# One 512-column matmul for the two that share a tile's high weights

## The chip, the core and the metric

The kernel runs on one core of a Trainium2 chip. The metric is device time in microseconds (us) of one execution. PE is TensorE, DVE is VectorE, ACT is ScalarE, POOL is GpSimd and SP is the engine that issues the loads. The core has an SBUF for tiles and a PSUM of banks of 512 fp32 columns, into which TensorE writes its products.

## The reference

Two blocks of a language model over 256 tokens of width 2048. The first holds a pooling layer and a sparse-attention layer, the second one attention layer of three kinds of heads and a gated feed-forward layer of width 5632. All inputs and outputs are fp32. Most of the arithmetic is in projections of this kind:

```python
h = rmsnorm(x, norm_g)
proj = h @ w_in                                   # 2048 x 4096 and more
return x + jnp.concatenate([y_pool, y_mem], -1) @ w_out
...
hid = silu(dwconv(h @ w_gate)) * (h @ w_up)       # 2048 x 5632 each
x = x + hid @ w_down
```

## The kernel before

Activations stand transposed: 16 blocks of 128 features by T = 256 tokens. A weight comes as 699 units of up to 128x1024 fp32 (8 blocks of 128x128). Each unit passes a stage: SP loads it into one of four slots (`s_stage`), ACT rounds it to fp32r (`s_wh`, line 1059), and DVE subtracts to get the low part (`s_wl`, line 1574). There are three slots for each of the two parts, so ACT waits until TensorE is done with the unit three before. Every activation block has a high and a low part too, `R[:, 0, k, :]` and `R[:, 1, k, :]` (`s_rh`, `s_ry`, `s_hid`). A product is then the sum of three matmuls of 256 columns per block (lines 490 to 492): high weights with high activations, high weights with low ones, low weights with high ones. I call the three matmuls of one 128x128 weight block a k-tile.

Most output tiles have two units, so 16 k-tiles, and lie in one of two PSUM banks (`psg`) in turn; groups of four tiles use two banks more (`pst`). In the residual stages (`wo0`, `wo1`, `wo2`, `wd`) some first tiles (4, 8, 12 and 2 of 16) go in passes: one pass takes one unit of each of these tiles, the next pass the other. `pair` computes values with 512 moving columns (lines 549 to 551) and isn't touched by the change except that it waits for both banks.

DVE takes every tile out of its bank: `scaled` (lines 1620 and 1622) multiplies it with the row norm, `add` (line 1793) adds it to the residual `X`. The order on each engine is written out by hand: `nxt()` runs one step of the side jobs and then one split of a unit. In the last pass of a residual stage DVE's order for each tile is add, low part of the new activation (line 1592), split of a unit; ACT's is high part (line 1071), rounding of a unit. `held` and `vacant` make TensorE wait for the bank until the tile that lay in it has been taken out (semaphore `out`). POOL sums squares of X for the norms (lines 2263 to 2270; for `wo1` also 2512 to 2519) and builds the windows of the compressed keys (line 2343).

Of the kernel before, what the change touches and what calls it, by code (L numbers as in the profile page):

```python
# [466 lines left out]


def both(R):
    return lambda k: (R[:, 0, k, :], R[:, 1, k, :])  # L470


def tensor_program(e, S, P, M):
# [4 lines left out]
    def vacant(*banks):  # L478

        for b in banks:  # L480
            if b in held:
                w.wait_ge(*held[b])

    def unit():
        done[0] += 1
        side.tick()

    def three(o, wh, wl, x, first, last):
        xh, xl = x
        e.matmul(o, wh, xh, start=first, stop=False)  # L490
        e.matmul(o, wh, xl, start=False, stop=False)  # L491
        return e.matmul(o, wl, xh, start=False, stop=last)  # L492

    def ready(name, base=0):
        return lambda k: w.wait_ge(name + "l", base + k + 1)

    def b_unit(o, nk, k0, first, last, x, ready, mw=128):
        c = done[0]
        r = c % NR
        w.wait_ge("wl", c + 1)  # L500
        for kk in range(nk):
            ws = slice(kk * mw, kk * mw + mw)
            ready(k0 + kk)
            m = three(o, M.WH[:, r, ws], M.WL[:, r, ws], x(k0 + kk), first and kk == 0, last and kk == nk - 1)
        m.then_inc(S["units"], 1)

    def tile(t, x, ready, sizes=(8, 8), k0=0, mw=128):

        bank = P.bank[t]
        vacant(bank)  # L510
        held[bank] = P.out[t]
        k = k0
        for n, nk in enumerate(sizes):
            b_unit(M.product(bank)[0:mw, 0:T], nk, k, n == 0, n == len(sizes) - 1, x, ready, mw)
            k += nk
            if n == len(sizes) - 1:
                assert done[0] + 1 == P.end[t], t
            unit()

    def group(tiles, x, ready, hook=None):  # L520

        for n in range(2):
            for p, t in enumerate(tiles):
                if n == 0:
                    vacant(P.bank[t])
                    held[P.bank[t]] = P.out[t]
                b_unit(M.product(P.bank[t])[:, 0:T], 8, 8 * n, n == 0, n == 1, x, ready)
                if hook is not None and n == 0 and p == 3:
                    hook()
                unit()  # L530

    def pair(t, x, ready):

        banks = [P.bank[t, i] for i in range(2)]
        vacant(*banks)
        for i in range(2):
            held[banks[i]] = P.out[t, i]
        for u in range(8):
            c = done[0]
            r = c % NR  # L540
            w.wait_ge("wl", c + 1)
            steps = [(kk, i) for i in range(2) for kk in range(2)] if u == 7 else [(kk, i) for kk in range(2) for i in range(2)]
            for n, (kk, i) in enumerate(steps):
                k = 2 * u + kk
                ready(k)
                xh, xl = x(k)
                ts, ws = slice(128 * i, 128 * i + 128), slice(512 * kk, 512 * kk + 512)
                o = M.product(banks[i])
                e.matmul(o[:, :], xh[:, ts], M.WH[:, r, ws], start=(k == 0), stop=False)  # L549
                e.matmul(o[:, :], xh[:, ts], M.WL[:, r, ws], start=False, stop=False)  # L550
                m = e.matmul(o[:, :], xl[:, ts], M.WH[:, r, ws], start=False, stop=(k == 15))  # L551
                if u == 7 and n == 1:
                    m.then_inc(S["half"], 1)
            m.then_inc(S["units"], 1)
            unit()

    def residual(name, x, ready, order=(0, 1), early=4, sizes=(8, 8)):
        at = [sum(sizes[:m]) for m in range(len(sizes))]
        for n, m in enumerate(order):
            for j in range(early):  # L560
                tile((name, j) if n == len(order) - 1 else (name, "part", m, j), x, ready, (sizes[m],), at[m])
        for j in range(early, KT):
            tile((name, j), x, ready, sizes)
# [69 lines left out]
    def pool_group(g):  # L633
        for i in range(3):
            tile(("z", 3 * g + i), H0, ready("h0"))
        for a, nt in ((0, 2), (2, 1)):
            c = done[0]
            r = c % NR
            w.wait_ge("wl", c + 1)
            w.wait_ge("rpl", g + 1)  # L640
            for i in range(a, a + nt):
                bank = ("t", 0) if i == 2 else ("o", i)
                o = M.PST[:, 0, 0:T] if i == 2 else M.PSO[i][:, 0:T]
                vacant(bank)
                for k in range(3):
                    ws = slice(((i - a) * 3 + k) * 128, ((i - a) * 3 + k + 1) * 128)
                    m = three(o, M.WH[:, r, ws], M.WL[:, r, ws], (M.RP[g % 2][:, 0, k, :], M.RP[g % 2][:, 1, k, :]), k == 0, k == 2)
                if i == 0:
                    m.then_inc(S["wp0"], 1)
                held[bank] = ("y_w", YAT["pool"] + 3 * g + i + 1)  # L650
            m.then_inc(S["units"], 1)
            if a == 2:
                side.tick()
            unit()
# [226 lines left out]
    def diff_head(h):  # L881
# [149 lines left out]
    for hv in range(2):  # L1031
        first = 22 * hv
        if hv == 0:
            group([(n, j) for j in range(2) for n in ("wg", "wu")], Y, ready("hf"), ffn_hook)
            first = 2
        for j in range(first, 22 * hv + 22):
            tile(("wg", j), Y, ready("hf"))
            tile(("wu", j), Y, ready("hf"))
        residual(("wd", hv), both(M.HID), ready("hid", 22 * hv), (0, 1, 2), 2, (8, 7, 7))
# [523 lines left out]
def vector_program(e, S, P, M):  # L1563
# [12 lines left out]
    def nxt(n=1):  # L1576
        for _ in range(n):
            side.tick()
            split()

    def chain(ins):

        ins.then_inc(S["dve"], 1)
        chained[0] += 1

    def link():
        w.wait_ge("dve", chained[0])
# [25 lines left out]
    def whole(t):  # L1613
        w.wait_ge("units", P.end[t])
        return M.product(P.bank[t])

    def scaled(t, dst, scale, rb):

        if scale is None:
            e.tensor_tensor(dst, whole(t)[:, 0:T], M.RB[rb][:, :], ALU.mult).then_inc(S["out"], 1)  # L1620
        else:
            e.scalar_tensor_tensor(dst, whole(t)[:, 0:T], scale, M.RB[rb][:, :], ALU.mult, ALU.mult).then_inc(S["out"], 1)

    def tiles(name, n, dst, scale, rb):
        for j in range(n):
# [18 lines left out]
    def silu(*t):  # L1644
        i = ZAT[t]
        yield
        yield
        w.wait_ge("z_t", i + 1)
        if t[0] == "zm":
            dst = (M.ZS0, M.ZS1)[t[1]][t[2] % 4]  # L1650
        else:
            dst = M.ZS0[t[1] % 4] if t[0] == "z" else M.ZS1[t[1] % 4]
        e.scalar_tensor_tensor(dst[:, :], M.ET[i % 2][:, :], 1.0, M.ZT[i % 2][:, :], ALU.add, ALU.mult).then_inc(S["z_d"], 1)

    def gate(rb, *t):

        nxt()
        i = ZAT[t]
        if i >= 2:
            w.wait_ge("z_d", i - 1)  # L1660
        e.scalar_tensor_tensor(M.ZT[i % 2][:, :], whole(t)[:, 0:T], 0.5, M.RB[rb][:, :], ALU.mult, ALU.mult).then_inc(S["out"], 1)
        side.start(silu(*t))
        nxt()

# [125 lines left out]

    def add(t, j):

        e.tensor_tensor(M.X[:, j, :], whole(t)[:, 0:T], M.X[:, j, :], ALU.add).then_inc(S["out"], 1)  # L1793

    def residual(name, post, order=(0, 1), early=4, units=2, begin=None):
        for n, m in enumerate(order):
# [85 lines left out]
    def gates():  # L1882
        yield
        yield
        w.wait_ge("gt_act", 1)
        gf = M.GT[:, :, :].rearrange("p t c -> p (t c)")
        chain(e.tensor_scalar(gf, gf, 1.0, None, ALU.add))
        link()
        e.reciprocal(gf, gf).then_inc(S["gts"], 1)
# [166 lines left out]
    side.start(mem_norm())  # L2056
    nxt(4)
    for j in range(4):
        e.tensor_copy(M.MK0[:, j, :], whole(("mk", 0, j))[:, 0:T]).then_inc(S["out"], 1)
        nxt()  # L2060
    v_pair(("mv", 0), M.MV0[:, 0, :], 0, "mem_c")
    side.start(x_low())
# [59 lines left out]
        if j % 2:  # L2122
            side.start(rope_pair(5 + j // 2, M.QN, j))
    w.wait_ge("hct", 2)
    e.tensor_tensor(M.ZT[0][0:36, :], whole("gate")[0:36, 0:T], M.RB[0][0:36, :], ALU.mult).then_inc(S["out"], 1)
    side.start(gates())
    nxt()
    for j in range(4):
# [71 lines left out]
    for hv in range(2):  # L2200
        first = 22 * hv
        if hv == 0:
# [9 lines left out]
            first = 2  # L2212
# [22 lines left out]
    for n, (a, b) in enumerate(((0, 1), (1, 3), (3, 6), (6, 9), (9, 11))):  # L2235
        w.wait_ge("xg", b)
        for j in range(a, b):
            x = e.tensor_tensor(M.X[:, j, :], M.X[:, j, :], M.RB[1][:, :], ALU.mult)
# [490 lines left out]
```

## Time and profile before

| | us |
|---|---|
| three runs, median (lowest to highest) | 2176.29 (2176.24 to 2177.77) |
| the profiled execution, its own time | 2176.39 |
| its span in the profile | 2174.6 |
| PE busy | 2123.9 |
| DVE busy | 1272.6 |
| ACT busy | 990.4 |
| POOL busy | 575.1 |

A matmul's record of some 284 ns overlaps the next ones, so the busy time of PE says only that it had work; the pace is read from the starts of two matmuls. Times of rows are from the span's start.

### The profile page before, as it was taken

To read this page: it belongs to the slowest core of one execution; us is meant where nothing else is said; L and a number is where in the kernel's file an instruction comes from. 1 tells how busy PE (TensorE), PEld (TensorE's weight loads), DVE (VectorE), ACT (ScalarE), POOL (GpSimd) and SP (SyncE) were. 2 spreads that over 40 slices of the span, in tenths; PEclk is the share of its full clock that TensorE was granted. 3 is DMA by queue.
4 is the path that set the end of the run, shared out by engine and by line. 5 is a ranking of instruction groups with operands and counts; after the bars stand their busy time and mean duration, and the time that the engine had idled before them with its cause. 6 is when DMAs were issued, how large, how long until landed. Compare 5 with 4: busy or idle time off the path is not lost.

```text
span 2174.6 us, 38858 instructions
## 1 busy us (share of the span) xinstructions
PE 2123.9 (98%) x16462; PEld 2040.3 (94%) x16462; DVE 1272.6 (59%) x1667; ACT 990.4 (46%) x1428; POOL 575.1 (26%) x551
## 2 busy tenths in 40 slices
PE   7999999999899999989999999999999999999997
PEld 7899999998799999989978899999999999999997
DVE  8855665566655545656545556666555455655544
ACT  5544444444532545433455454454444334444443
POOL 8214442233400244691121122311110001111122
PEclk9999999999999999999999999999999999999998
DMA  7554555556654433565554445656656665655664
GB/s 251 174 184 146 188 181 191 176 178 190 192 180 125 134 107 109 167 197 171 157 162 140 127 135 160 191 180 181 184 184 180 180 192 182 181 183 183 180 181 133
DMA packets 104126, 370.61 MB, mean 170 GB/s; under 512 B 11633, under 2 KB 12945, under 8 KB 103825
## 3 DMA queue, kind: packets, MB, share of 16 engines
q1 hardware_dynamic: 103952, 368.13, 54.5%
q8 instruction: 130, 2.13, 0.4%
q14 instruction: 44, 0.35, 0.0%
HBM read 365.98 MB, written 2.10 MB: 169 GB/s over the span
## 4 chain that ended last, share of the span: by engine, by line
PE 88%; POOL 6%; DVE 3%; ACT 1%; issue 1%; DMA 0%; SPq 0%; DVEq 0%; POOLq 0%; ACTq 0%
PE psg L490 24%; PE psg L491 24%; PE psg L492 24%; POOL s_zf L2343 2%; PE psg L549 2%; PE psg L550 2%; PE psg L551 2%; DVE s_wl L1574 1%; POOL s_psq L2267 1%; POOL s_psq L2512 1%; PE pst L492 1%; PE pst L491 1%; PE pst L490 1%; POOL s_psq L2517 1%; PE pst L586 1%
## 5 line engine op out<-in xcount | busy, mean ns | idle before, releaser
L1574 DVE TENSOR_TENSOR s_wl<-s_stage,s_wh 128x1024 fp32r<-128x1024 f32 (+3 forms) x699 | 864.9, 1239 | 553.9 <-ACT s_wh L1059 551.8
L1059 ACT ACTIVATE s_wh<-s_stage 128x1024 fp32r<-128x1024 f32 (+3 forms) x699 | 726.3, 1041 | 774.9 <-PE psg L492 686.7
L490 PE MATMUL psg<-s_ry,s_wh 128*128 128x256 f32 x2672 | 765.0, 286 | 2.9 <-DVE s_mv L1635 2.5
L491 PE MATMUL psg<-s_ry,s_wh 128*128 128x256 f32 x2672 | 757.9, 284 | 0.0
L492 PE MATMUL psg<-s_ry,s_wl 128*128 128x256 f32 x2672 | 757.7, 284 | 0.0
L490 PEld LDWEIGHTS psg<-s_ry,s_wh 128*128 128x128 f32 x2672 | 513.5, 192 | 11.7 <-issue 5.5
L491 PEld LDWEIGHTS psg<-s_ry,s_wh 128*128 128x128 f32 x2672 | 513.4, 192 | 0.5
L492 PEld LDWEIGHTS psg<-s_ry,s_wl 128*128 128x128 f32 x2672 | 513.3, 192 | 0.1
L490 PE MATMUL psg<-s_rh,s_wh 128*128 128x256 f32 x1280 | 369.8, 289 | 12.4 <-DVE s_rh L1592 10.2
L492 PE MATMUL psg<-s_rh,s_wl 128*128 128x256 f32 x1280 | 363.8, 284 | 0.0
L491 PE MATMUL psg<-s_rh,s_wh 128*128 128x256 f32 x1280 | 363.8, 284 | 0.0
L490 PEld LDWEIGHTS psg<-s_rh,s_wh 128*128 128x128 f32 x1280 | 247.0, 193 | 17.1 <-issue 11.3
L491 PEld LDWEIGHTS psg<-s_rh,s_wh 128*128 128x128 f32 x1280 | 247.2, 193 | 0.4
L492 PEld LDWEIGHTS psg<-s_rh,s_wl 128*128 128x128 f32 x1280 | 247.1, 193 | 0.0
L2426 POOL TENSOR_TENSOR s_hid<-s_hh,s_hid 128x256 fp32r<-128x256 f32 x44 | 64.5, 1465 | 575.9 <-ACT s_hid L1397 575.9
L490 PE MATMUL psg<-s_hid,s_wh 128*128 128x256 f32 x704 | 199.2, 283 | 0.0
L491 PE MATMUL psg<-s_hid,s_wh 128*128 128x256 f32 x704 | 199.2, 283 | 0.0
L492 PE MATMUL psg<-s_hid,s_wl 128*128 128x256 f32 x704 | 199.2, 283 | 0.0
L490 PEld LDWEIGHTS psg<-s_hid,s_wh 128*128 128x128 f32 x704 | 135.2, 192 | 0.0
L491 PEld LDWEIGHTS psg<-s_hid,s_wh 128*128 128x128 f32 x704 | 135.2, 192 | 0.0
L492 PEld LDWEIGHTS psg<-s_hid,s_wl 128*128 128x128 f32 x704 | 135.2, 192 | 0.0
L2267 POOL TENSOR_TENSOR s_psq<-s_x 128x256 f32<-128x256 f32 x74 | 58.4, 789 | 165.0 <-DVE s_x L1793 162.8
(378 smaller groups left out, 2388.5 us busy)
## 6 DMA issues: line engine op xcount, KB each, us to landing
s_stage<-in_wo SPq DMA_DIRECT2D x96, 512.0 KB, 3.4
s_stage<-in_wg SPq DMA_DIRECT2D x88, 512.0 KB, 3.5
s_stage<-in_wu SPq DMA_DIRECT2D x88, 512.0 KB, 3.5
s_stage<-in_ain SPq DMA_DIRECT2D x64, 512.0 KB, 3.3
s_stage<-in_wd SPq DMA_DIRECT2D x64, 448.0 KB, 3.4
s_stage<-in_wkv SPq DMA_DIRECT2D x32, 512.0 KB, 3.7
s_stage<-in_wd SPq DMA_DIRECT2D x32, 512.0 KB, 3.6
s_stage<-in_bq SPq DMA_DIRECT2D x24, 512.0 KB, 3.5
```

What stands on the lines that cost most here:

```text
L490: e.matmul(o, wh, xh, start=first, stop=False)
L491: e.matmul(o, wh, xl, start=False, stop=False)
L492: return e.matmul(o, wl, xh, start=False, stop=last)
L549: e.matmul(o[:, :], xh[:, ts], M.WH[:, r, ws], start=(k == 0), stop=False)
L550: e.matmul(o[:, :], xh[:, ts], M.WL[:, r, ws], start=False, stop=False)
L551: m = e.matmul(o[:, :], xl[:, ts], M.WH[:, r, ws], start=False, stop=(k == 15))
L586: m = e.transpose(M.PST[:, h, b:b + 128], src[:, a:a + 128], ident)
L1059: e.activation(M.WH[:, c % NR, 0:n], M.ST[:, c % NS, 0:n], ACT.Copy).then_inc(S["wh"], 1)
L1574: e.tensor_tensor(M.WL[:, c % NR, 0:n], M.ST[:, c % NS, 0:n], M.WH[:, c % NR, 0:n], ALU.subtract).then_inc(S["wl"], 1)
L2267: chain(e.tensor_tensor(b, src, src, ALU.mult))
L2343: x = e.tensor_scalar(dst, Z[:, :, l:l + 16 * 14 + 1:16], M.vec("pe", 32 * v + l), None, ALU.add)
L2426: e.tensor_tensor(M.HID[:, 1, i, :], M.HH[j % 2][:, :], M.HID[:, 0, i, :].bitcast(F32), ALU.subtract).then_inc(S["hidl"], 1)
```

## The change

The high and low parts of an activation block are taken as one moving operand of two runs of 256 columns, so that the high weights are used in one matmul of 512 columns. It fills both halves of a bank: columns 0 to 255 get high by high, 256 to 511 high by low. The low weights' matmul of 256 columns adds to the second half. In the last k-tile of a tile it comes first, so that the wide one ends the tile. DVE adds the halves: `scaled` by a reduction over pairs of columns that lie 256 apart, then the multiplication as a second instruction that waits for the first; `add` by two additions in a row.

```diff
 def both(R):
-    return lambda k: (R[:, 0, k, :], R[:, 1, k, :])
+    return lambda k: (R[:, 0, k, :], R[:, :, k, :], R[:, 1, k, :])
...
-            m = three(o, M.WH[:, r, ws], M.WL[:, r, ws], x(k0 + kk), first and kk == 0, last and kk == nk - 1)
+            xh, xx, _ = x(k0 + kk)
+            begin, end = first and kk == 0, last and kk == nk - 1
+            if end:
+                e.matmul(o[:, T:2 * T], M.WL[:, r, ws], xh, start=False, stop=False)
+            m = e.matmul(o, M.WH[:, r, ws], xx, start=begin, stop=end)
+            if not end:
+                m = e.matmul(o[:, T:2 * T], M.WL[:, r, ws], xh, start=False, stop=False)
         m.then_inc(S["units"], 1)
...
+    def summed(t, dst, rows=128):
+        return e.tensor_reduce(dst, whole(t)[0:rows, :].rearrange("p (s t) -> p t s", s=2), AX.X, ALU.add)
+
-    def scaled(t, dst, scale, rb):
+    def scaled(t, dst, scale, rb, rows=128):
+        chain(summed(t, dst, rows))
+        link()
         if scale is None:
-            e.tensor_tensor(dst, whole(t)[:, 0:T], M.RB[rb][:, :], ALU.mult).then_inc(S["out"], 1)
+            e.tensor_tensor(dst, dst, M.RB[rb][0:rows, :], ALU.mult).then_inc(S["out"], 1)
...
     def add(t, j):
-        e.tensor_tensor(M.X[:, j, :], whole(t)[:, 0:T], M.X[:, j, :], ALU.add).then_inc(S["out"], 1)
+        b = whole(t)
+        chain(e.tensor_tensor(M.X[:, j, :], b[:, T:2 * T], M.X[:, j, :], ALU.add))
+        link()
+        e.tensor_tensor(M.X[:, j, :], b[:, 0:T], M.X[:, j, :], ALU.add).then_inc(S["out"], 1)
...
-        e.tensor_copy(M.MK0[:, j, :], whole(("mk", 0, j))[:, 0:T]).then_inc(S["out"], 1)
+        summed(("mk", 0, j), M.MK0[:, j, :]).then_inc(S["out"], 1)
```

On PE, near the end of a tile of the first group (memory keys, stationary blocks of `s_wh` and `s_wl`, bank `pst`), the order before is:

```order
L490 MATMUL pst<-s_rh,s_wh 128x256
L491 MATMUL pst<-s_rh,s_wh 128x256
L492 MATMUL pst<-s_rh,s_wl 128x256
L490 MATMUL pst<-s_rh,s_wh 128x256
L491 MATMUL pst<-s_rh,s_wh 128x256
L492 MATMUL pst<-s_rh,s_wl 128x256
```

and now:

```order
L508 MATMUL pst<-s_rh,s_wh 128x512
L510 MATMUL pst<-s_rh,s_wl 128x256
L508 MATMUL pst<-s_rh,s_wh 128x512
L510 MATMUL pst<-s_rh,s_wl 128x256
L507 MATMUL pst<-s_rh,s_wl 128x256
L508 MATMUL pst<-s_rh,s_wh 128x512 x2
```

A k-tile has two matmuls instead of three; at the tile's end two narrow ones stand in a row, then the wide one of this tile and the wide one of the next.

On DVE, in the last pass of the stage `wo2` (one unit per tile), the order before is:

```order
L1793 TENSOR_TENSOR s_x<-psg,s_x 128x256
L1592 SCALAR_TENSOR_TENSOR s_ry<-s_x,s_vec,s_ry 128x256
L1574 TENSOR_TENSOR s_wl<-s_stage,s_wh 128x1024
L1793 TENSOR_TENSOR s_x<-psg,s_x 128x256
L1592 SCALAR_TENSOR_TENSOR s_ry<-s_x,s_vec,s_ry 128x256
```

and now:

```order
L1806 TENSOR_TENSOR s_x<-psg,s_x 128x256
L1808 TENSOR_TENSOR s_x<-psg,s_x 128x256
L1598 SCALAR_TENSOR_TENSOR s_ry<-s_x,s_vec,s_ry 128x256
L1580 TENSOR_TENSOR s_wl<-s_stage,s_wh 128x1024
L1806 TENSOR_TENSOR s_x<-psg,s_x 128x256
L1808 TENSOR_TENSOR s_x<-psg,s_x 128x256
```

Each tile has one addition more ahead of the low part and the split.

## Rows read from the trace of the kernel before

**Rows 1.** The page: the span and busy times.

```profile
span 2174.6 us, 38858 instructions
PE 2123.9 (98%) x16462; PEld 2040.3 (94%) x16462; DVE 1272.6 (59%) x1667; ACT 990.4 (46%) x1428; POOL 575.1 (26%) x551
```

**Rows 2.** The page: shares of the chain that ended last, by engine.

```profile
PE 88%; POOL 6%; DVE 3%; ACT 1%; issue 1%; DMA 0%; SPq 0%; DVEq 0%; POOLq 0%; ACTq 0%
```

**Rows 3.** Groups by line, PE, line 490: name, shapes, count, busy us, mean ns, idle.

```profile
L490 PE MATMUL psg<-s_ry,s_wh 128*128 128x256 f32 x2672 | 765.0, 286 | 2.9 <-DVE s_mv L1635 2.5 <-DVE s_vcc L1635 0.4
L490 PE MATMUL psg<-s_rh,s_wh 128*128 128x256 f32 x1280 | 369.8, 289 | 12.4 <-DVE s_rh L1592 10.2 <-DVE s_wl L1574 2.0
L490 PE MATMUL psg<-s_hid,s_wh 128*128 128x256 f32 x704 | 199.2, 283 | 0.0
L490 PE MATMUL pst<-s_ry,s_wh 128*128 128x256 f32 x96 | 27.4, 285 | 0.0
L490 PE MATMUL pst<-s_rh,s_wh 128*128 128x256 f32 x64 | 18.1, 283 | 0.0
```

**Rows 4.** Instructions in time, PE, 256 columns: start us, length us, what.

```profile
999.77 0.28 PE L490 MATMUL psg<-s_ry,s_wh 128*128 128x256 f32 x1
...
1002.65 0.28 PE L490 MATMUL psg<-s_ry,s_wh 128*128 128x256 f32 x1
```

**Rows 5.** Instructions in time, PE, 512 columns.

```profile
92.90 0.39 PE L551 MATMUL psg<-s_wh,s_ry 128*128 128x512 f32 x1
...
94.94 0.39 PE L551 MATMUL psg<-s_wh,s_ry 128*128 128x512 f32 x1
```

**Rows 6.** Groups by line and shape, DVE.

```profile
L1620 DVE TENSOR_TENSOR s_uu<-psg,s_rb 128x256 f32<-128x256 f32 x43 | 18.2, 424 | 24.1 <-PE psg L492 24.1
L1744 DVE TENSOR_REDUCE s_stat<-pss 128x2 f32<-128x512 f32 x20 | 13.6, 680 | 0.0
L2046 DVE TENSOR_TENSOR s_hh<-s_uu,s_cv 128x256 f32<-128x256 f32 x44 | 18.3, 415 | 0.0
L1686 DVE TENSOR_TENSOR s_mk<-s_mk,s_rb 128x256 f32<-128x256 f32 x4 | 3.4, 894 | 0.0
```

**Rows 7.** Instructions in time, DVE, two that wait for one another.

```profile
977.91 0.42 DVE L1598 SCALAR_TENSOR_TENSOR s_nw<-pso,s_rb 128x256 f32<-128x256 f32 x1 [10.76 <-ACT s_rb L1078]
978.37 0.42 DVE L1600 SCALAR_TENSOR_TENSOR s_nw<-s_nw,s_rb 128x256 f32<-128x256 f32 x1
```

**Rows 8.** Stretches of time: busy us and count of each engine, clock, DMA.

```profile
20.00:30.00 10.00, 9.43 (x79) 9.23 (x77) 10.00 (x12) 6.33 (x11) 9.53 (x13) 1.00 0.58 207
1500.00:1550.00 50.00, 50.00 (x419) 50.00 (x418) 29.17 (x39) 23.14 (x30) 6.75 (x5) 1.00 0.60 183
```

**Rows 9.** Instructions in time, DVE, last pass of `wo2`.

```profile
1344.74 0.42 DVE L1793 TENSOR_TENSOR s_x<-psg,s_x 128x256 f32<-128x256 f32 x1 [0.57 <-PE psg L492]
...
1347.84 0.42 DVE L1793 TENSOR_TENSOR s_x<-psg,s_x 128x256 f32<-128x256 f32 x1
1348.83 0.48 DVE L1592 SCALAR_TENSOR_TENSOR s_ry<-s_x,s_vec,s_ry 128x256 fp32r<-128x256 f32 x1 [0.58 <-ACT s_ry L1071]
1349.78 1.23 DVE L1574 TENSOR_TENSOR s_wl<-s_stage,s_wh 128x1024 fp32r<-128x1024 f32 x1 [0.46 <-ACT s_wh L1059]
...
1378.69 0.41 DVE L1793 TENSOR_TENSOR s_x<-psg,s_x 128x256 f32<-128x256 f32 x1
```

**Rows 10.** Instructions in time, POOL: the first square of `wo1`.

```profile
889.81 0.61 POOL L2263 TENSOR_TENSOR s_acc<-s_x 128x256 f32<-128x256 f32 x1 [7.05 <-DVE s_x L1793]
```

**Rows 11.** Instructions in time, PE: the norm after `wo1`.

```profile
974.87 1.19 PE L569 MATMUL pso<-s_acc,s_one 128*128 128x256 f32 x2 [7.26 <-issue]
```

**Rows 12.** Chain that ended last, in order of time: the windows of the compressed keys.

```profile
480.37 3.77 POOL s_zf L2343 x4
484.16 0.64 ACT s_zb L1216
484.82 0.70 DVE s_zb L1846
485.61 4.36 POOL s_zf L2343 x4
```

**Rows 13.** Instructions in time, PE: a `pair` behind a tile.

```profile
1014.18 0.47 PE L549 MATMUL psg<-s_wh,s_ry 128*128 128x512 f32 x1 [0.56 <-DVE s_kcc L1620]
```

More of the change, by code:

```diff
@@ L513, in tile @@
         for n, nk in enumerate(sizes):
-            b_unit(M.product(bank)[0:mw, 0:T], nk, k, n == 0, n == len(sizes) - 1, x, ready, mw)
+            b_unit(M.product(bank)[0:mw, :], nk, k, n == 0, n == len(sizes) - 1, x, ready, mw)
             k += nk
@@ L526, in group @@
                     held[P.bank[t]] = P.out[t]
-                b_unit(M.product(P.bank[t])[:, 0:T], 8, 8 * n, n == 0, n == 1, x, ready)
+                b_unit(M.product(P.bank[t])[:, :], 8, 8 * n, n == 0, n == 1, x, ready)
                 if hook is not None and n == 0 and p == 3:
@@ L545, in pair @@
                 ready(k)
-                xh, xl = x(k)
+                xh, _, xl = x(k)
                 ts, ws = slice(128 * i, 128 * i + 128), slice(512 * kk, 512 * kk + 512)
@@ L1615, in whole @@
         return M.product(P.bank[t])
-    def scaled(t, dst, scale, rb):
+    def summed(t, dst, rows=128):
[3 more added lines that the diff above has]
+        link()
         if scale is None:
-            e.tensor_tensor(dst, whole(t)[:, 0:T], M.RB[rb][:, :], ALU.mult).then_inc(S["out"], 1)
+            e.tensor_tensor(dst, dst, M.RB[rb][0:rows, :], ALU.mult).then_inc(S["out"], 1)
         else:
-            e.scalar_tensor_tensor(dst, whole(t)[:, 0:T], scale, M.RB[rb][:, :], ALU.mult, ALU.mult).then_inc(S["out"], 1)
+            e.scalar_tensor_tensor(dst, dst, scale, M.RB[rb][0:rows, :], ALU.mult, ALU.mult).then_inc(S["out"], 1)
     def tiles(name, n, dst, scale, rb):
@@ L1660, in gate @@
             w.wait_ge("z_d", i - 1)
-        e.scalar_tensor_tensor(M.ZT[i % 2][:, :], whole(t)[:, 0:T], 0.5, M.RB[rb][:, :], ALU.mult, ALU.mult).then_inc(S["out"], 1)
+        scaled(t, M.ZT[i % 2][:, :], 0.5, rb)
         side.start(silu(*t))
@@ L2124, in vector_program @@
     w.wait_ge("hct", 2)
-    e.tensor_tensor(M.ZT[0][0:36, :], whole("gate")[0:36, 0:T], M.RB[0][0:36, :], ALU.mult).then_inc(S["out"], 1)
+    scaled("gate", M.ZT[0][0:36, :], None, 0, 36)
     side.start(gates())
```

## The prediction, made before the changed kernel ran

> **What bounds the kernel now.** I read the page's busy times first [rows 1]: PE has work in 98% of the span, DVE in 59%, ACT in 46%. Then the chain of waits [rows 2]: 88% of it is PE, 6% POOL, 3% DVE. So TensorE's pace is the bound, and the few places where the chain is on POOL or DVE are those where a faster TensorE gains nothing. Next I read that pace in the instructions in order of time. Eight k-tiles, 24 matmuls of 256 columns, take 1002.65 - 999.77 = 2.88 us [rows 4], 120.0 ns each. Nine matmuls of 512 columns take 94.94 - 92.90 = 2.04 us [rows 5], 226.7 ns each. 256 columns more cost 106.7 ns, so a matmul is 0.4167 ns per column and 13.3 ns besides. That the line through two points gives exactly a column per cycle of the 2.4 GHz level speaks for reading the 13.3 ns as a price per matmul, each with weights of its own.
>
> **The gain on TensorE.** The change touches 2672 + 1280 + 704 + 96 + 64 = 4816 k-tiles [rows 3]. Each was 3 x 120.0 = 360.0 ns and becomes 226.7 + 120.0 = 346.7 ns. The columns are the same 768; one matmul with its weight load goes. That is 13.3 ns per k-tile, 0.107 us per unit of eight, 64.2 us in all if TensorE never waits longer than before. The trace has no wide matmul whose moving operand lies in two runs far apart, and none between narrow ones. Its cost is bounded by what it replaces: at most two narrow ones (240.0 ns, gain nil); at the other end by the columns alone (213.3 ns, gain 26.7 ns per k-tile, 128 us). I take 226.7 ns, the row of the same width.
>
> Here a page speaks against the change. The Trainium skill, "TensorE: Matmul & The Clock Gate", section "Back-to-back issue gap", puts a warm matmul at N/2.4 + 2.5 ns; by that a k-tile would go from 327.5 to 325.0 ns, and the sum would be a gain of 12 us, an estimate. The rows differ from it at both widths, 120.0 and 226.7 ns, and I go by the rows.
>
> **The cost on DVE.** Of the 317 added DVE instructions 205 are in `scaled` and 112 in `add`. A `scaled` was one instruction of 0.42 us; now a reduction of 512 PSUM columns, nearest row 0.68 us, and a multiplication in SBUF of 0.42 us [rows 6]. Instructions that wait for one another start 0.46 us apart when 0.42 us long [rows 7], so a link adds 0.04 us: 1.14 us instead of 0.42. That is 0.72 us more for each, 148 us in all. An `add` gets 0.46 us more: 52 us. In the feed-forward stage DVE is busy 29.17 of 50 us [rows 8], 3.4 us per tile of 5.76 us; it becomes 4.1 of 5.55 us. The bank is freed some 0.7 us later with a whole tile's 5.55 us of room. So this is hidden behind TensorE in the long stages. The reduction's shape is unknown (256 sums of two, 256 columns apart): below it can't be under the 0.42 us of one reading of 256 columns, above I bound it at three times the row, 2.0 us; even that gives 5.5 us per tile and just fits.
>
> The multiplication now reads two SBUF tensors. Of that form one row has 415 ns and one, at the start where POOL is 9.5 us of 10 busy, 894 ns [rows 6, 8]. The Trainium skill, "SBUF — State Buffer", section "Who interferes with whom", says that a DVE instruction with two SBUF inputs contends with a POOL instruction that reads SBUF. By that rule, the trace agrees, and `add`, with one input in PSUM, is spared.
>
> **Where it isn't hidden.** (a) The last pass of `wo2`: 12 tiles of one unit. Adds are 3.085 us apart, (1378.69 - 1347.84)/10 [rows 9], more than a unit's 2.88: add, ACT's high part, ACT's rounding, DVE's split and the next add follow one another. The first add of the pass had waited for TensorE by 0.57 us, so the slack was being eaten but lasted. Now the period is 3.085 + 0.46 = 3.545 us, against a unit of 2.77. Behind the add stand the low part and the split, and TensorE waits for the bank: tile 12 of the stage can start when add 10 is done, 0.57 + 10 x 3.545 + 0.90 = 36.9 us after the end of tile 0, where TensorE alone would need 11 x 2.773 = 30.5. I charge 6.1 us, leaving 0.3 for what it lacked before. In `wo0` with four such tiles the same sum gives 0.3.
>
> (b) `wo1`: POOL squares from 889.81 to TensorE's norm at 974.87, before which TensorE idles 7.26 us [rows 10, 11]. POOL sets this stretch. The gain of its 27 units (7 of the last pass, 16 of the tiles behind, 4 of the group) is lost, 2.9 us, and its first square starts 0.46 us later. The same lag as in (a), for eight tiles, is inside that idle time.
>
> (c) The start: from 20 to 30 us DVE is busy 10.00 of 10 us [rows 8], and I take it for the bound of the whole first group. Its 64 k-tiles gain nothing, 0.85 us, and the four reductions in place of copies add 4 x 0.26 = 1.0.
>
> (d) The compressed keys: a loop of POOL, ACT, DVE of 485.61 - 480.37 = 5.24 us [rows 12] sets the pace. About seven units gain nothing, 0.75, and DVE's longer queue and POOL's sharing may add 1.0.
>
> (e) `pair` behind a tile waits for the bank, 0.56 us [rows 13]; two such places get 0.72 us more each: 1.5.
>
> (f) The last add, ahead of the final norm: 0.46.
>
> (g) Places with slack under a microsecond that I can't see before, most of all around the last heads where DVE and ACT wait for one another: 2, between 0 and 10.
>
> The sum: 0.3 + 6.1 + 2.9 + 0.46 + 0.85 + 1.0 + 0.75 + 1.0 + 1.5 + 0.46 + 2 = 17.3 us. 64.2 - 17.3 = 46.9 us. The profiled execution took 2176.39 us, the span 2174.6 and 1.8 around it, and the median of the runs is 2176.29: 2176.4 - 46.9 = 2129.5, so I forecast 2130 us.
>
> **The rivals.** *DVE hides less.* If the reduction is much over 0.68 us or the splits come late in the attention stages, another 8 to 30 us of waits appear. For it: DVE runs its list in order, and the splits stand behind the longer `scaled`. Against: in the feed-forward stage DVE keeps over a quarter of its time free. The time would be 2138 to 2160.
>
> *The price isn't per matmul.* If most of the 13.3 ns is a wait that the sequence of narrow and wide keeps, and a k-tile saves only a fifth of it, 2.7 ns, the gain is 13 us. The stalls, with a period of 3.545 against a unit of 2.86, are some 12: 2175. For it stands that both widths were measured only among their own kind. A gain of this size is what the page named above would give.
>
> *The wide matmul's weights come late (slower).* Its weights must be loaded under a narrow matmul, and its operand lies in two runs. If the pair of matmuls then takes 360 ns or more, nothing is gained, and what stays are the costs of DVE: (a) 36.9 against 11 x 2.88 = 31.7, so 4.9 more; 0.46, 1.0, 1.0, 1.5, 0.46 and 2: about 11 us slower, 2188. It decides from 357.7 ns per k-tile on (11 us / 4816 = 2.3 ns). Against: before, too, every load lies under a narrow matmul at 120 ns.
>
> *The reduction bounds (slower).* At 3 us it would make a feed-forward tile 6.5 us, (6.5 - 5.76) x 88 = 65 us over before for these alone, less about 20 us gained in the residual stages: 2220. It decides from about 2.6 us.
>
> **Chances.** Forecast 0.78 (its own range 2117 to 2138); DVE hides less 0.11; the price isn't per matmul 0.04, three quarters of it within 0.2% and one slower; late weights 0.04; reduction 0.03. A measurement of this kernel tells 0.2%, 4.4 us, from no change. Faster 0.78 + 0.11 = 0.89, same 0.03, slower 0.01 + 0.04 + 0.03 = 0.08. The range is 2117, with few of the waits of (a) to (g) and a little more gain, to 2144, which takes in the nearer part of the second case.
>
> **What would show it.** Starts of narrow and wide matmul 120 and 227 ns apart, a k-tile of 0.347 us; 9632 matmuls in `tile` and `group` instead of 14448. DVE busy about 1470 us, the reduction 0.68 us. Adds of the last pass of `wo2` 3.5 us apart with TensorE waiting for them; an idle time before the norm of `wo1` that is shorter by the lag of its last pass but ends as late after the first square, 85 us. A k-tile of 0.36 us, or a reduction of over 2 us, would make it wrong.

## The result, and the profile after

The changed kernel takes 2157.61 us (median of four runs, 2157.39 to 2158.88), the kernel before 2176.49 beside it: a ratio of 0.9913, interval 0.9896 to 0.993. It is 18.9 us faster, where 46.9 were forecast; 2157.6 lies outside the range of 2117 to 2144. The page of its profiled execution, span and busy times, against [rows 1], and the chain that ended last, against [rows 2]:

```profile
span 2155.6 us, 29543 instructions
PE 2092.7 (97%) x11646; PEld 1775.3 (82%) x11646; DVE 1456.3 (68%) x1984; ACT 996.9 (46%) x1428; POOL 570.1 (26%) x551
PE 84%; POOL 6%; DVE 5%; issue 2%; ACT 2%; DMA 0%; DVEq 0%; SPq 0%; POOLq 0%; ACTq 0%
```

4816 matmuls are gone (16462 to 11646) and DVE has 184 us more work, near the forecast's 200. The chain, third line, is still PE's with 84% in place of 88% [rows 2]. So TensorE's pace is what to read next: instructions in order of time on PE, start and length in us.

```profile
1502.19 0.40 PE L508 MATMUL psg<-s_ry,s_wh 128*128 128x512 f32 x1
1502.42 0.28 PE L510 MATMUL psg<-s_ry,s_wl 128*128 128x256 f32 x1
1502.54 0.40 PE L508 MATMUL psg<-s_ry,s_wh 128*128 128x512 f32 x1
...
1505.37 0.40 PE L508 MATMUL psg<-s_ry,s_wh 128*128 128x512 f32 x1
```

Nine k-tiles from 1502.19 to 1505.37 are 3.18 us, 353.3 ns each. The forecast had 346.7, before it was 360.0 [rows 4]. I call a matmul of 512 columns wide and one of 256 columns narrow. Over the whole trace a wide matmul takes 235.4 ns from its start to the next one's (mean of 4633), a narrow one 117.1 (4784); starts with a wait or another pause behind them are left out, so the two add up to a little less than 353.3. The wide one is 8.7 ns slower than 226.7 [rows 5], the narrow one 2.9 ns faster than 120.0. The gain per k-tile is 6.7 ns, half of what was forecast: 4816 x 6.7 = 32.3 us. Of these 18.9 arrive; the difference of 13.4 us is waits.

DVE's groups by line and shape (name, shapes, count, busy us, mean ns, idle and its releaser), against [rows 6]:

```profile
L1625 DVE TENSOR_REDUCE s_uu<-psg 128x256 f32<-128x512 f32 x43 | 29.8, 692 | 21.9 <-PE psg L508 21.9
L1632 DVE TENSOR_TENSOR s_uu<-s_uu,s_rb 128x256 f32<-128x256 f32 x44 | 18.7, 424 | 1.5
L1806 DVE TENSOR_TENSOR s_x<-psg,s_x 128x256 f32<-128x256 f32 x112 | 47.3, 422 | 35.1 <-PE psg L508 35.0
L1808 DVE TENSOR_TENSOR s_x<-psg,s_x 128x256 f32<-128x256 f32 x112 | 47.6, 425 | 3.8
```

The reduction takes 692 ns (forecast 680), the multiplication 424, the second addition 425. In the feed-forward stage DVE has room left, the stretch as in [rows 8]:

```profile
1500.00:1550.00 50.00, 50.00 (x285) 43.38 (x284) 36.49 (x49) 24.60 (x32) 5.53 (x5) 1.00 0.62 190
```

36.49 of 50 us, and PE never idle. The last pass of `wo2`, DVE and then PE, against [rows 9]:

```profile
1345.33 0.42 DVE L1808 TENSOR_TENSOR s_x<-psg,s_x 128x256 f32<-128x256 f32 x1
...
1348.88 0.42 DVE L1808 TENSOR_TENSOR s_x<-psg,s_x 128x256 f32<-128x256 f32 x1
...
1352.42 0.42 DVE L1808 TENSOR_TENSOR s_x<-psg,s_x 128x256 f32<-128x256 f32 x1
```

```profile
1349.36 0.50 PE L508 MATMUL psg<-s_rh,s_wh 128*128 128x512 f32 x1 [0.47 <-DVE s_x L1808]
1352.90 0.50 PE L508 MATMUL psg<-s_rh,s_wh 128*128 128x512 f32 x1 [0.46 <-DVE s_x L1808]
```

The second additions are 3.545 us apart, as forecast, and TensorE waits for each. Around `wo1` the first square on POOL and the norm on PE, against [rows 10, 11]:

```profile
879.34 0.62 POOL L2278 TENSOR_TENSOR s_acc<-s_x 128x256 f32<-128x256 f32 x1 [7.34 <-DVE s_x L1808]
```

```profile
966.26 1.19 PE L575 MATMUL pso<-s_acc,s_one 128*128 128x256 f32 x2 [7.33 <-issue]
```

That is 86.92 us, before it was 85.06. And the list of PE's waits (us in all, times, longest), for [rows 13]:

```profile
PE psg L508 <- DVE s_x L1808: 5.9, 12, 0.9
PE psg L555 <- DVE s_kb L1632: 1.3, 1, 1.3
PE psg L555 <- DVE s_kcc L1632: 1.3, 1, 1.3
```

One place stands out, on DVE and on POOL, just behind this norm:

```profile
973.57 3.27 DVE L1634 SCALAR_TENSOR_TENSOR s_qc<-s_qc,s_rb 128x256 f32<-128x256 f32 x1
```

```profile
971.00 5.56 POOL L2401 TENSOR_TENSOR s_bt<-s_bt,s_csc 128x2048 f32<-128x2048 f32 x1
```

The added multiplication reads two SBUF tensors, and beside this long POOL instruction it takes 3.27 us in place of 0.42. The prediction named such a clash and gave it no price. Of the 205 multiplications only two more take over 430 ns (497 and 644). In the kernel before, another DVE instruction with two SBUF inputs took 3.01 us beside the same POOL instruction (at 982.18), so most of this stall isn't new.

### The profile page after: what moved, and what is told of

It is laid out like the page before. It is cut to its first block, busy times and chain, and to the rows that moved or that the text cites. A ratio compares the mean times of both kernels' runs of the same rounds, so it can differ in the third digit from the quotient of the medians.

```text
span 2155.6 us, 29543 instructions
## 1 busy us (share of the span) xinstructions
PE 2092.7 (97%) x11646; PEld 1775.3 (82%) x11646; DVE 1456.3 (68%) x1984; ACT 996.9 (46%) x1428; POOL 570.1 (26%) x551
## 4 chain that ended last, share of the span: by engine, by line
PE 84%; POOL 6%; DVE 5%; issue 2%; ACT 2%; DMA 0%; DVEq 0%; SPq 0%; POOLq 0%; ACTq 0%
PE psg L508 46%; PE psg L510 22%; POOL s_zf L2358 2%; DVE s_wl L1580 2%; PE psg L555 2%; PE psg L557 2%; PE psg L556 2%; PE psg L507 1%; PE pst L508 1%; ACT s_wh L1065 1%; POOL s_acc L2534 1%; POOL s_psq L2282 1%; POOL s_psq L2527 1%; PE pst L592 1%; DVE s_rh L1598 1%
## 5 line engine op out<-in xcount | busy, mean ns | idle before, releaser
L508 PE MATMUL psg<-s_ry,s_wh 128*128 128x512 f32 x2672 | 946.5, 401 | 3.4 <-DVE s_mv L1647 2.5
L510 PE MATMUL psg<-s_ry,s_wl 128*128 128x256 f32 x2501 | 703.3, 281 | 0.0
L508 PEld LDWEIGHTS psg<-s_ry,s_wh 128*128 128x128 f32 x2672 | 493.7, 188 | 119.1 <-issue 6.7
L508 PE MATMUL psg<-s_rh,s_wh 128*128 128x512 f32 x1280 | 461.9, 405 | 19.2 <-DVE s_rh L1598 9.2
L508 PEld LDWEIGHTS psg<-s_rh,s_wh 128*128 128x128 f32 x1280 | 238.1, 189 | 79.5 <-issue 13.0
L508 PE MATMUL psg<-s_hid,s_wh 128*128 128x512 f32 x704 | 245.9, 399 | 0.0
L508 PEld LDWEIGHTS psg<-s_hid,s_wh 128*128 128x128 f32 x704 | 129.7, 188 | 29.0
L2285 POOL TENSOR_TENSOR s_acc<-s_acc,s_psq 128x256 f32<-128x256 f32 x89 | 88.3, 993 | 7.0
L1806 DVE TENSOR_TENSOR s_x<-psg,s_x 128x256 f32<-128x256 f32 x112 | 47.3, 422 | 35.1 <-PE psg L508 35.0
L555 PE MATMUL psg<-s_wh,s_ry 128*128 128x512 f32 x160 | 64.5, 403 | 3.6 <-DVE s_kb L1632 1.3
```

What stands on the lines that cost most here:

```text
L508: m = e.matmul(o, M.WH[:, r, ws], xx, start=begin, stop=end)
L510: m = e.matmul(o[:, T:2 * T], M.WL[:, r, ws], xh, start=False, stop=False)
L1806: chain(e.tensor_tensor(M.X[:, j, :], b[:, T:2 * T], M.X[:, j, :], ALU.add))
L2285: e.tensor_tensor(acc, acc, b, ALU.add).then_inc(S[name], 1)
```

## The experiments

Runs of a label's own group stood beside runs of the kernel before on the same chip, 2177.1 to 2177.9 us. Times are medians in us, ratios are to the kernel before, with a 95% interval. "In a row" means among matmuls of the same width. A pace is the mean time from one matmul's start to the next one's over a whole trace, in ns, without the starts that a wait or a pause follows.

### Is it DVE or the pace? (e3, e4)

e3 keeps the halves and DVE's work, but makes the matmuls narrow:

```diff
-            m = e.matmul(o, M.WH[:, r, ws], xx, start=begin, stop=end)
+            e.matmul(o[:, 0:T], M.WH[:, r, ws], xh, start=begin, stop=False)
+            e.matmul(o[:, T:2 * T], M.WH[:, r, ws], xl, start=False, stop=False)
+            m = e.matmul(o[:, T:2 * T], M.WL[:, r, ws], xh, start=False, stop=end)
```

> The changed kernel's DVE with the three narrow matmuls of before, of which the first writes columns 0 to 255 of the bank and the other two columns 256 to 511. It shows what the added DVE instructions cost by themselves. The forecast's list (without what a faster TensorE loses) gives 4.9 for the last pass of wo2, 0.5 + 1.0 + 1.0 + 1.5 + 0.5 for wo1's start, the first group, the compressed keys, the pairs and the end, 2 for the rest: 11 us, 2188 us. If DVE's work is more in the way than the list says: 2192 us or more. If it is all hidden: 2176 us.

2188.19 us, ratio 1.005 (1.0033 to 1.0066), 120.0 ns per matmul. DVE's added work alone costs 10.7 us; the prediction's third rival had that sum at 11 (below it is said which of its terms were off).

e4 keeps the wide matmuls, and DVE reads only the first half of the bank with the instructions of before (the second half's products are left out of the result):

```diff
-        chain(summed(t, dst, rows))
-        link()
+        src = whole(t)[0:rows, 0:T]
...
-        chain(e.tensor_tensor(M.X[:, j, :], b[:, T:2 * T], M.X[:, j, :], ALU.add))
-        link()
```

> The changed kernel's matmuls with the DVE instructions of before: each tile is taken out with one instruction that reads columns 0 to 255 alone, so the second half of the sum is left out of the result. It shows what TensorE gives by itself. At 353.3 ns per k-tile the gain is 4816 x 6.7 = 32 us, less 27 units of wo1 (1.4), the compressed keys (0.4) and the first group (0.4): 2147 us. If the missing 28 us of the forecast lie with DVE and not with the pace: under 2140 us.

2144.26, 0.9847 (0.9832 to 0.9861), with 353 ns per k-tile: 33.2 us less than the kernel before, where the changed kernel has 18.9. The pace gives 32 to 33 us, and DVE's added work takes 11 (e3) to 14 (e4) back. So the forecast's costs stand, its gain doesn't.

### Is it the second run of columns? (e1, e2)

```diff
-        self.RY = alloc(all_, "ry", [128, 2, KT, T], F32R)
+        self.RY = alloc(all_, "ry", [128, KT, 2, T], F32R)[:, :, :, 0:T].rearrange("p k s t -> p s k t")
```

and the same for `s_rh` and `s_hid`. e2 has `T + 8` in place of the allocation's last `T`.

> The changed kernel with the high and low part of each activation block side by side in SBUF, so that the wide matmul reads one run of 512 columns instead of two runs of 256. In the changed kernel a k-tile takes 353 ns (wide 235, narrow 118) where 346.7 was forecast. Theory A, the second run of the moving operand costs some 8 ns: the wide matmul falls to 227 ns, a k-tile to 347, 4816 x 6.6 ns = 32 us less TensorE time, of which POOL, DVE and the compressed keys keep some 3: 2129 us. Theory B, the price lies in a wide matmul between narrow ones, or in the weights it loads: k-tile and time stay, 2157 us. Theory C, a matmul that writes both halves of a bank while DVE reads the other bank is slowed: 2157 us too.

> As the run with the parts side by side, but with 8 unused columns (32 bytes) behind each part, so that the wide matmul reads two runs that lie 32 bytes apart instead of 16 KB or more. Theory A1, each second run costs, however near: 235 ns for the wide matmul and 2157 us as the changed kernel. Theory A2, only the far jump costs: 227 ns, 2129 us. Theory B: 2157 us.

e1: 2156.54, 0.9905 (0.989 to 0.9919), wide 235.3, k-tile 353: theory A fails, two runs far apart cost nothing here. e2: 2147.55, 0.9861 (0.9846 to 0.9876), which no theory had expected. Its trace:

```profile
1501.51 0.39 PE L508 MATMUL psg<-s_ry,s_wh 128*128 128x512 f32 x1
...
1503.61 0.39 PE L508 MATMUL psg<-s_ry,s_wh 128*128 128x512 f32 x1
```

Six k-tiles in 2.10 us: 350.0 ns, wide 231.1, narrow 118.2. 32 unused bytes are worth 9 us against e1, so the place of the operand counts.

### Is it the alternation of widths? (e5, e9, e6, e7, e8, e11)

e5 sorts the matmuls of a unit:

```diff
-        for kk in range(nk):
+        wide, narrow = [(kk, 1) for kk in range(nk)], [(kk, 0) for kk in range(nk)]
+        for kk, both_ in (wide[:1] + narrow + wide[1:] if last else wide + narrow):
```

> In each unit the eight wide matmuls stand in a row, then the eight narrow ones (in a tile's last unit the first wide one, the narrow ones, the other wide ones). Same matmuls, same operands, same addresses; fewer changes between widths. Theory of the alternation (a wide one that follows a narrow one, or is followed by one, costs 8.6 ns more than among its own kind): wide 226.7, narrow 120.0, k-tile 347 ns, the time 2157.6 less 30 = 2128 us. Rival, the operand's addresses: wide 235, k-tile 353 to 355, the time 2157 to 2163. Rival, two wide ones in a row get their weights worse than one under a narrow one: wide over 236, the time above 2163.

2141.78, 0.9843 (0.9829 to 0.9858): half of the 30 us that the theory of the alternation expected. e9 has only two changes per tile:

```diff
-        for kk, both_ in (wide[:1] + narrow + wide[1:] if last else wide + narrow):
+        for kk, both_ in (wide + narrow if first and not last else wide[:1] + narrow + wide[1:] if first else narrow + wide):
```

> As e5_grouped, but a tile's second unit starts with its narrow matmuls, so that a whole tile has 8 wide ones, 16 narrow ones, 8 wide ones, and the next tile goes on with wide ones: two changes of width per tile instead of four. e5_grouped showed 226.7 and 120.0 ns in a row and up to 242 after a change. Theory of the alternation: most of the 2 ns per k-tile that e5_grouped still lacked to 346.7 come back, 2141.8 less 5 to 9 = 2133 to 2137 us. Rival, the 242 ns belong to the place in the unit and not to the change of width: 2141 to 2143.

2142.56, 0.984 (0.9825 to 0.9855). Groups in order of time, start, length and count:

```profile
1500.73 3.82 PE L507 MATMUL psg<-s_ry,s_wh 128*128 128x512 f32 x16
1504.38 2.08 PE L509 MATMUL psg<-s_ry,s_wl 128*128 128x256 f32 x16
1506.30 1.09 PE L507 MATMUL psg<-s_ry,s_wh 128*128 128x512 f32 x4
```

Sixteen narrow ones take 1.92 us, 120 ns each. Sixteen wide ones take 3.65, 228.1: over the whole trace the first five behind narrow ones need 233.5, 235.7, 228.5, 232.4 and 230.8 ns, the other eleven 226.7. The first narrow one behind wide ones takes 113.8, the later ones 119 to 120. So a change to wide costs 27 ns in all, a change back returns 7; it takes five wide matmuls until the pace of [rows 5] is back, and with alternating widths it never is. Sorting gives back 15 us of what was missing. Fewer changes in e9 brought nothing over e5, its expectation of 5 to 9 us failed: the paces are nearly the same (wide 229.1 and 229.5, narrow 119.3 and 119.2), as e5 too has only one run of slow wide ones per tile besides its lone wide one, which takes 233.3.

e6 is e5's order in e2's layout, e7 is e2 with `T + 16`, e8 puts `T + 8` into the far layout of the changed kernel:

> The order of e5_grouped together with the activations' layout of e2_gap8 (parts side by side with 32 bytes unused behind each). Alternation: like e5_grouped, 2128 us, the gap brings nothing more. Addresses: like e2_gap8, wide 231, 2147 to 2153. If both act apart from each other, wide under 231 and the time below both of these.

> As e2_gap8 but with 64 bytes unused behind each part instead of 32. If the gain of e2_gap8 grows as parts move away from multiples of 1 KB: wide below 231, the time 2140 to 2147. If only an odd multiple of 32 bytes matters: wide 235, the time 2156. If any gap does the same: wide 231, 2147.

> The changed kernel's layout (all high parts, then all low parts) with 32 bytes unused behind each block. The two runs of a wide operand are still 16 or 22 blocks apart. If the address of each block matters and not the distance of the two runs: wide 231, the time 2147. If only a gap between the two runs of adjacent parts helps: wide 235, 2157.

e6: 2154.04, 0.9894 (0.9877 to 0.991). e7: 2148.71, 0.9871 (0.9856 to 0.9885), wide 231.9, narrow 117.9. e8: 2155.02, 0.9898 (0.9883 to 0.9913), 233.3 and 117.5. In e7 any gap did the same, its third case; e8 lies between its two cases and bears out neither. In e6 sorting did harm, and the trace shows where:

```profile
1501.24 3.65 PE L507 MATMUL psg<-s_ry,s_wh 128*128 128x512 f32 x15
1504.73 1.10 PE L509 MATMUL psg<-s_ry,s_wl 128*128 128x256 f32 x8
```

3.49 us for fifteen: 232.7 ns in a row, where the original layout has 226.7, while the narrow ones take 117.6. With the gap wide ones in a row lose and narrow ones gain; both causes act, but they don't add up as the expectation had it. e11 looked whether one run of 512 columns (a gap only behind it) does better in e9's order:

```diff
+        self.RY = alloc(all_, "ry", [128, KT, 2 * T + 8], F32R)[:, :, 0:2 * T].rearrange("p k (s t) -> p s k t", s=2)
```

> The order of e9_two_changes; the two parts of a block lie side by side without a gap (one run of 512 columns) and 32 bytes are unused behind each pair of parts. Theory: the first column's address alone sets the pace, and off the multiple of 1 KB a narrow one is 117.7 ns (seen in e6_grouped_gap8) and a wide one 224: k-tile 342, the time 2111 to 2120 us. Rival, off that multiple a wide one is 232.5 whether or not a gap lies in its middle: k-tile 350, 2150 to 2155. Rival, the gap in the middle made it slow: wide 227, narrow 118, k-tile 345, 2125 to 2132.

2158.98, 0.9916 (0.9901 to 0.9931): wide 233.0, narrow 119.0. The theory failed, and the gap in the middle isn't the cause either.

### Does the place act without wide matmuls? (e10, e13, e14, e16)

Here all is the kernel before. e10 has e2's layout.

> The kernel before (three matmuls of 256 columns per k-tile, DVE as before) with the layout of e2_gap8. Theory that the layout alone acts on every matmul: 117.7 ns instead of 120.0, 14448 x 2.3 ns = 33 us less, 2144 us, near the best of the kernels with wide matmuls. Rival, it acts only where widths are mixed: 120.0 ns, 2177 us.

2139.99, 0.9826 (0.9812 to 0.9841). The kernel before gets 38 us faster by 32 unused bytes, twice the gain of the change:

```profile
1500.02 0.28 PE L490 MATMUL psg<-s_ry,s_wh 128*128 128x256 f32 x1
...
1502.82 0.28 PE L490 MATMUL psg<-s_ry,s_wh 128*128 128x256 f32 x1
```

Eight k-tiles in 2.80 us: 350.0 ns for three matmuls, the very time of e2 for two. Since e2 has the added DVE work besides, it is some 8 us slower than e10.

The program's addresses show what the gap moves. In a partition `s_wh` starts at byte 32896, `s_wl` at 45184, `s_ry` at 92800, `s_rh` and `s_hid` at 125568. Each is 128 bytes behind a multiple of 256, and so is each block in them. I call that the common distance. e13 adds a constant:

```diff
-        self.RY = alloc(all_, "ry", [128, 2, KT, T], F32R)
+        self.RY = alloc(all_, "ry", [128, 2 * KT * T + 8], F32R)[:, 8:2 * KT * T + 8].rearrange("p (s k t) -> p s k t", s=2, k=KT)
```

The 8 is 64 in e14 and 16 in e16; since `s_rh` and `s_hid` lie behind `s_ry`, they move by twice as much.

> The kernel before, with its activations shifted by a constant: s_ry starts 32 bytes later, s_rh and s_hid 64 bytes later. In the kernel before the first column of every weight block and of every activation part lies 128 bytes behind a multiple of 512 bytes. Theory of the phase (weights and activations at the same distance cost each other time): 117 ns or less in place of 120.0, the time 2130 to 2142 us. Rival, only a distance that changes from block to block helps, as in e10_before_gap8: 120.0 ns, 2177.

> The same with s_ry 256 bytes later and s_rh and s_hid 512 bytes later, which is the old distance again. Theory of the phase in 512 bytes: s_ry's matmuls (8600 of 14448) get faster, those of s_rh and s_hid stay at 120.0 ns; 8600 x 3 ns = 26 us less, 2151. Rival, only the lower bits of the address count: 120.0 everywhere, 2177. Rival, a phase in 1024 bytes: all of them faster, 2135 to 2142.

> The kernel before, s_ry 64 bytes later and s_rh and s_hid 128 bytes later. In e13_before_shift32 s_ry took 117.1 ns at 32 bytes and s_hid 113.3 and s_rh 117.6 at 64. If the distance sets the pace: s_ry 113 to 117 at 64 bytes and another value for s_rh and s_hid at 128, the time 2115 to 2140 us. If any distance that isn't a multiple of 256 does the same: 117 for all, 2137 to 2142. If 128 bytes are the old state again: s_rh and s_hid 120.0, about 2150.

| | s_ry moved, pace | s_rh moved, pace | s_hid, pace | us | ratio |
|---|---|---|---|---|---|
| e13 | 32 bytes, 117.1 | 64, 117.6 | 113.3 | 2136.38 | 0.9811 (0.9797 to 0.9826) |
| e14 | 256, 119.9 | 512, 119.9 | 120.0 | 2177.11 | 1.0 (0.9991 to 1.001) |
| e16 | 64, 117.7 | 128, 119.1 | 118.7 | 2155.75 | 0.9909 (0.9893 to 0.9926) |

A constant shift does it, and 256 or 512 bytes do nothing: these five shifts fit a dependence on the place modulo 256. That is the theory of the phase, with 256 in place of the 512 that I had written. e16 came out as none of its cases: `s_ry` at 64 bytes takes 117.7, as `s_rh` did at 64 in e13, and 128 bytes are neither the old state nor as good as 32 or 64. (`s_ry` has 8304 of the 14448 matmuls, not 8600 as one expectation says.)

`pair`, whose code no experiment touches, turns the same way: where the weights move past `s_ry` or `s_rh` as stationary operand, its wide matmuls take 228.5 ns before and in e14, and 232.6 to 233.2 in e10, e13 and e16. Narrow ones are faster off the common distance, wide ones on it. Why, no run tells. Nor does any run tell the distance between the two operands from the place of the activations by itself: the weights never moved, and no run moved both by the same number of bytes. One trace speaks against the place of the moving operand alone. In the kernel before, where `s_zb` (32 bytes off the common distance) is stationary, the moving operand is `s_wh` at its old place, and these narrow matmuls take 118.1 ns and not 120.

### What is left of the change (e15, e12, e17, e18)

e15 is the changed kernel with e13's shift. e12 is e9 with the matmuls and the single addition of before in the last passes of `wo0`, `wo1` and `wo2`:

```diff
+        if slim:
+            for kk in range(nk):
+                ready(k0 + kk)
+                xh, _, xl = x(k0 + kk)
+                m = three(o[:, 0:T], M.WH[:, r, kk * mw:kk * mw + mw], M.WL[:, r, kk * mw:kk * mw + mw], (xh, xl), kk == 0, kk == nk - 1)
+            m.then_inc(S["units"], 1)
+            return
```

> The changed kernel with the shift of e13_before_shift32. If the phase acts, both kernels land where their number of matmuls doesn't matter, as with the gap of 32 bytes (350 ns per k-tile in e2_gap8 and e10_before_gap8): 2147 to 2150 us. Rival, the shift leaves the pace: 2157.

> e9_two_changes, and in the last pass of wo0, wo1 and wo2 (4, 8 and 12 tiles of one unit) the three narrow matmuls and the single add of the kernel before. It takes DVE's lag away where TensorE waited for it: in wo2 6.1 less 0.3 us come back by the prediction, 24 units pay 0.1 us each, of which those of wo2 and wo1 are hidden; wo1 stays bound by POOL but its first square comes 0.46 us earlier. 4 to 7 us less than e9_two_changes, 2128 to 2132 us. Rival, the stall of wo2 is given back later by another wait (the norm behind it): within 2 us of e9_two_changes.

e15: 2146.92, 0.9863 (0.9846 to 0.9879), wide 230.9 and narrow 118.5 on average. With the same shift the kernel before (e13) takes 2136.38, 10.5 us less: off the common distance the change brings no pace, and DVE's added work stays. e12: 2134.36, 0.9801 (0.9785 to 0.9817), 8.2 us less than e9, more than the 4 to 7 expected. The stretch from POOL's first square to the norm of `wo1` shows the part that I had missed (PE in e12, then POOL):

```profile
961.36 1.19 PE L581 MATMUL pso<-s_acc,s_one 128*128 128x256 f32 x2 [8.92 <-issue]
```

```profile
876.30 0.61 POOL L2287 TENSOR_TENSOR s_acc<-s_x 128x256 f32<-128x256 f32 x1 [6.88 <-DVE s_x L1813]
```

85.06 us again, as before the change, against 87.20 in e9 and 86.92 in the changed kernel.

e17 is e12 with e13's shift. e18 is e12 with `s_rh` and `s_hid` 64 bytes later and the three narrow matmuls in the whole down projection.

> e12_narrow_passes with the shift of e15_shift32. If off the common distance the matmuls' number doesn't matter, a k-tile takes 347 to 350 ns in any order: 2134 to 2145 us, no better than e12_narrow_passes or e13_before_shift32. If wide ones in a row keep 227 and narrow ones go to 117: k-tile 344, 2118 to 2124 us. Rival as in e6_grouped_gap8, wide ones in a row get slower off the common distance (232.6): 2140 to 2150 us.

> e12_narrow_passes with s_rh and s_hid 64 bytes later (s_ry stays) and, in the down projection, the three narrow matmuls and the single add of the kernel before. Paces seen so far: s_hid three narrow ones at 64 bytes 3 x 113.3 = 340 ns (e13_before_shift32) for 348.8 in e12_narrow_passes; s_rh 116.8 + 229.7 = 346.5 (e17_changes_shift32) for 349.0; s_ry as it was. If they add up: 704 x 8.8 + 1280 x 2.5 ns = 9.4 us less than e12_narrow_passes, 2125 us, and the best of all. Rival, the pace of s_hid at 64 bytes came from the state of the queue in that kernel: 347 ns there, 2130 to 2134 us.

e17: 2135.02, 0.981 (0.9795 to 0.9824). Narrow 116.8, wide in a row 233.2 on `s_ry` and 229.6 on `s_rh` and `s_hid`: what one gains the other loses. e18: 2133.84, 0.9801 (0.9787 to 0.9814), equal to e12. Its `s_hid` lies at the same byte as in e13, its matmuls there are the same three, and yet they take another time (e13, then e18):

```profile
1699.76 0.28 PE L490 MATMUL psg<-s_hid,s_wh 128*128 128x256 f32 x1
...
1701.80 0.28 PE L490 MATMUL psg<-s_hid,s_wh 128*128 128x256 f32 x1
```

```profile
1699.93 0.28 PE L490 MATMUL psg<-s_hid,s_wh 128*128 128x256 f32 x1
...
1701.69 0.28 PE L490 MATMUL psg<-s_hid,s_wh 128*128 128x256 f32 x1
```

Six k-tiles in 2.04 us, 340.0 ns, and five in 1.76, 352. The rival was right about the pace, if not its size (347): the distance alone doesn't fix it, and what else does is open. e12 and e18 are the fastest medians, 43 us below the kernel before. But a shift of 32 and 64 bytes in the kernel before (e13) gives 41 of these, and the intervals of e12 and e13 overlap: no run shows that the merged matmuls beat the shifted kernel.

## Why the prediction was wrong, point by point

**The gain: wrong, and this is the step.** "I take 226.7 ns, the row of the same width" failed. That row is of wide matmuls in a row at the common distance. Between narrow ones a wide one takes 235.4; sorted it is 226.7 again once five have passed (e5, e9). The trace of before showed this already, in the five matmuls ahead of [rows 5]. The first line is the first wide one behind narrow ones, the last is the one with which [rows 5] begins:

```profile
91.74 0.40 PE L549 MATMUL psg<-s_wh,s_ry 128*128 128x512 f32 x1
...
92.90 0.39 PE L551 MATMUL psg<-s_wh,s_ry 128*128 128x512 f32 x1
```

Five take 1.16 us, 232 ns each, without any wait between them; the row began right behind the slow ones. With it fell the reading that 13.3 ns are "a price per matmul". The time of a k-tile over the 320.0 ns of its 768 columns is 40.0 for three narrow ones at the common distance and 30 off it (e10); for two matmuls it is 33.3 as changed, 30 with e2's gap and 28.5 sorted (e9). The same number of matmuls has several prices, and three can be as cheap as two. The price goes by how the widths follow one another and where the operands lie. The term of 64.2 us measured 32.3; e4, where DVE's work is as before, gains 33.2.

The page that spoke against the change, the Trainium skill's "TensorE: Matmul & The Clock Gate", section "Back-to-back issue gap", gives N/2.4 + 2.5 ns as the gap of an isolated matmul; the prediction left that word out and used it for a stream. Its estimate of 12 us is 20 below the measured 32.3, the forecast's 64.2 is 32 above. No sequence here reached its 109.2 and 215.8 ns: the fastest paces were 113.3 and 226.7.

**The rival "the price isn't per matmul"** had the right kind of cause and the wrong size: it assumed a fifth of the saving, half came. It got 0.04, although I wrote that both widths were measured only among their own kind. The trace of before had a second hint: the matmuls on `s_zb`, narrow and at another place, start less than 120 ns apart, 118.1 on average of 165. In order of time:

```profile
505.02 0.28 PE L687 MATMUL pst<-s_wh,s_zb 128*128 128x256 f32 x1
...
506.09 0.28 PE L687 MATMUL pst<-s_wh,s_zb 128*128 128x256 f32 x1
```

Nine in 1.07 us. A straight line through two points looked exact (a column per cycle), and I took that for evidence. It was not.

**The costs: right in sum, and the sum is partly luck.** Forecast 17.3 with 13.3 ns per k-tile, 14.5 by the same list with 6.7 ns; measured 13.4 in the changed kernel, and 10.7 in e3 where the list had 11. For the single terms I take TensorE's lead: how much earlier the first matmul of a unit starts than in the kernel before. Units are counted over the 602 that the change touches; at 6.7 ns per k-tile each adds 0.054 us.

(a) The period of 3.545 is right. The lead falls from 10.7 us (unit 322) to 5.0 (332), where ten units should have added 0.5: 6.3 us lost. The forecast's sum with 2.827 us per unit gives 36.9 - 31.1 - 0.3 = 5.5. e3 loses 5.5 where the list had 4.9, so the term was 0.6 to 0.8 too low.

(b) "The same lag, for eight tiles, is inside that idle time" is wrong. The lead falls from 11.1 (unit 222) to 7.9 (249), where 27 units should have added 1.4: 4.7 us lost, where the forecast has 3.4 (1.9 with 6.7 ns). e3 loses 2.9 there, its list had 0.5. The squares come later with the adds, and POOL's stretch grows from 85.06 to 86.92 us. e12, with single adds, has 85.06 again.

(c) was too high. TensorE is 1.6 us behind at unit 8 and level at unit 9; at unit 20 the lead is 0.65 where 1.07 would be all: 0.4 lost, not 1.85.

(d) From unit 131 to 144, the stretch of [rows 12], the lead falls from 6.9 to 5.5 where 13 units should add 0.7: 2.1 us and not 1.75. In e3 1.7 us are lost there and 1.6 of them come back by unit 180.

(e) Two waits of 1.3 us in place of 0.56: 1.5, right. (f) TensorE's wait before the final norm grows from 1.02 to 1.48 us, the 0.46 forecast. (g) Of the 2 us some 0.6 can be named, a wait for a split near unit 90. So (a) and (b) were too low by over 3 us at the measured pace, (c) and (g) were too high, and part of (d) comes back; that these make up for one another was not foreseen.

**DVE** was right: 1.16 us for a `scaled` where 1.14 was forecast (mean of 205, the one of 3.27 us above among them), hidden in the feed-forward stage. *DVE hides less* came in a small part only: TensorE's waits for splits grew from 12.3 to 16.7 us. The two other rivals, the reduction as a bound and late weights with 360 ns, didn't come.

## What to carry to other kernels

A pace read from matmuls of one width in a row holds for that sequence at those addresses. Before a change that merges or mixes widths, read the first matmuls after a change of width too, compare the pace of all matmuls of the trace, and try a shift of the operands by 32 or 64 bytes first: here it gave 41 us without one instruction more. Merged matmuls paid most here in a row, at the common distance, and with the passes in which DVE sets the period left out; against the shifted kernel before they gained nothing that the runs can show.

## What the runs showed of the hardware

- A narrow fp32r matmul takes 120.0 ns when moving and stationary operands start at the same distance modulo 256 bytes, and 113.3 to 119.1 with the activations 32, 64 or 128 bytes from it (the weights stayed in place). A wide one in a row takes 226.7 at the common distance and 229.6 to 233.2 off it. The 113.3 came at 64 bytes in e13 only; with the same bytes e18 has 117.8.
- At the common distance a change from narrow to wide slows the next five wide matmuls by 2 to 9 ns each, 27 in all; the first narrow one behind wide ones is 6 ns faster (e9).
- All of this at the granted clock 1.00 of the stretches shown (2.4 GHz). The engines beside don't set it: over e3's trace, with DVE at 34.62 of 50 us where it was at 29.17 (1500 to 1550 us), the pace stayed 119.9.
- A reduction of 256 pairs that lie 256 columns apart in PSUM takes 692 ns, near the 680 of one of 512 columns to two sums [rows 6].
- A DVE instruction with two SBUF inputs took 3.27 us in place of 0.42 beside a POOL instruction of 5.56 us; beside most other POOL work it stayed at 0.42 to 0.43.
